# Two attentions of a fused two-block transformer kernel: implied waits dropped, and TensorE's wait for the scaled probabilities moved to the last score matmul

## Chip, cores and metric

One core of one Trainium2 chip. The time is the device time of one launch in microseconds (us), as the median of three runs. The aim of such work is a lower time.

## What is computed

The kernel runs two transformer blocks on a sequence of 1024 tokens of width 1024, all in fp32. Each block holds one attention, and the change touches only these two.

```python
def block_attention(q, k, v):            # first block: 8 query heads, 2 key/value heads of 64
    s = einsum('bqkgd,bskd->bkgqs', qi, k) * scale     # one block of 128 queries, all 1024 keys
    p = softmax(s, axis=-1)
    return einsum('bkgqs,bskd->bqkgd', p, v)
...
def _forgetting_attention(q, k, v, log_f):   # second block: 16 heads of 64, causal
    for blk in range(8):
        q0, q1 = blk * 128, (blk + 1) * 128
        s = einsum('bhqd,bhkd->bhqk', q[:, :, q0:q1], k[:, :, :q1]) * scale
        s = s + fcum[:, :, q0:q1, None] - fcum[:, :, None, :q1]
        s = where(kpos <= qpos, s, -inf)
        outs.append(einsum('bhqk,bhkd->bhqd', softmax(s), v[:, :, :q1]))
```

Around them stand the projections, a token MLP, a gated feed-forward layer with a convolution, and a state space branch.

## The kernel before

Every engine has its own instruction stream, written out by hand in a class of its own, and the streams meet only at semaphores. Each compute engine counts its finished steps up in one semaphore of its own: `pe_done`, `act_done`, `dve_done`, `pool_done`.
Both attentions (A = 1 and A = 2) are one loop over steps s, each of which takes one block of 128 queries of one head, called g. A head has eight blocks. In attention 1 there are 64 blocks of 1024 keys each. In attention 2 there are eight passes (p = 0 to 7) of two heads, so 16 blocks each, with g = 16 p + s, and block qt of a head has (qt + 1) x 128 keys.

One block goes through these steps:

1. `scores` on TensorE (L805, L806): the query tile times the high and the low part of the keys, 512 columns at a time, into one of two PSUM pairs (g % 2). In attention 2 a mask matmul (L810) ends it.
2. `top` on VectorE: the row maximum (L2573; in attention 2 L2568, then L2571 for the sign).
3. `soft` on ScalarE: the exponential with the row sum (L1645), then `soft` on VectorE: the reciprocal of the sum (L2581).
4. `weigh` on GpSimd (POOL, L3451): the probabilities times that reciprocal; its label is `weighed`.
5. `turn` on TensorE (L829): transposes of 128 x 128, at most four to a PSUM bank, so one or two halves. `turn` on ScalarE (L1660, label `phi`) takes a half out as the high part, and then `turn` on VectorE (L2596, label `plo`) as the low part, which frees the bank.
6. `back` on TensorE (L848), for two blocks together: probabilities times values; ScalarE (L1668) and VectorE (L2604) take the result out.

TensorE's order in step s is: `scores` of block s + 2, then, in attention 2, some chunks of a projection matmul as filler (L609 to L611, three matmuls of 512 columns each), then `turn` of block s, then, for every second s, `back` of blocks s - 1 and s - 2. GpSimd has other work in attention 2: it makes the low part of each weight tile (L3374), in its own program order.

Of the kernel before, what the change touches and what calls it, by code (L numbers as in the profile page):

```python
# [545 lines left out]
class TensorEngine(Engine):  # L546
# [243 lines left out]
        self.last_tails()  # L790
        self.mark("stage", "project1")

    def scores(self, A, g, h, qt, q, kh, kl, causal, ready):
        K = self.K
        nk = (qt + 1) * 128 if causal else 1024
        pair = g % 2
        qs = K.wrr(q)[:, qt * 128:(qt + 1) * 128]
        for half in range((nk + 511) // 512):
            c = slice(half * 512, min(nk, half * 512 + 512))
            out = K.ps[pair][:, c]  # L800
            diag = causal and c.stop == nk
            self.bank_free(2 * pair + half)
            for label in ready:
                self.wait_ge(*K.at(*label))
            self.op.matmul(out, qs, K.wrr(kh)[:, c], start=True, stop=False)  # L805
            t = self.op.matmul(out, qs, K.wrr(kl)[:, c], start=False, stop=not diag)  # L806
            if diag:
                self.consts()
                self.wait_ge(*K.at("maskr"))
                t = self.op.matmul(K.ps[pair][:, nk - 128:nk], K.idr[:, :], K.maskr[:, :],  # L810
                                   start=False, stop=True)
        t.then_inc(*self.done("scores", A, g))
        free = (("top", A, g),) if causal else (("top", A, g), ("exp", A, g))
        for half in range((nk + 511) // 512):
            self.emptied[2 * pair + half] = free

    def turn(self, A, g, qt, p, causal):
        K = self.K
        nk = qt + 1 if causal else 8
        par = g % 2 if nk <= 4 else 0  # L820
        self.consts()
        for half in range((nk + 3) // 4):
            bk = (half + par) % 2
            js = range(4 * half, min(nk, 4 * half + 4))
            self.wait_ge(*K.at("weighed", A, g))
            self.bank_free(4 + bk)
            for j in js:
                o = bk * 512 + (j - js[0]) * 128
                t = self.op.transpose(K.ps[2][:, o:o + 128], K.w(p)[:, j * 128:(j + 1) * 128],  # L829
                                      K.c_id)  # L830
            t.then_inc(*self.done("turn", A, g, half))
            self.emptied[4 + bk] = (("phi", A, g, half), ("plo", A, g, half))

    def back(self, A, g, qt, hi, lo, v, causal, ready):

        K = self.K
        nk = qt + 1 if causal else 8
        for gg in (g - 1, g):
            for half in range((((qt if gg == g else qt - 1) + 1 if causal else 8) + 3) // 4):
                self.wait_ge(*K.at("phi", A, gg, half))  # L840
                self.wait_ge(*K.at("plo", A, gg, half))
        for label in ready:
            self.wait_ge(*K.at(*label))
# [10 lines left out]
    def attend1(self):  # L854
        K = self.K

        def sc(s):
            h, qt = s // 8, s % 8
            k = 8 if h < 4 else 10
            self.scores(1, s, h, qt, h, k, k + 1, False, (("stacklo", "q", h // 2), ("stacklo", "q", 4),  # L860
                         ("stackhi2", "q", 4, 1)))

        for s in range(-2, 66):
            if s + 2 < 64:
# [356 lines left out]
    def attend2(self):  # L1221
        K = self.K
# [35 lines left out]
        for p in range(8):  # L1258
# [11 lines left out]
            def sc(s):  # L1270
                h = s // 8
                k = 2 + 2 * h
                self.scores(2, 16 * p + s, 2 * p + h, s % 8, h, k, k + 1, True,
                            (("stacklo", "q2", p, h), ("stacklo", "k", p, h),
                             ("stackhi2", "k", p, h)))

            for s in range(-2, 18):
                if s + 2 < 16:
# [97 lines left out]
class ScalarEngine(Engine):  # L1376
# [251 lines left out]
    def soft(self, A, g, qt, p, causal):  # L1628
# [1 line left out]
        nk = (qt + 1) * 128 if causal else 1024  # L1630
        m, den = (K.st[:, 4 * (g % 16) + j:4 * (g % 16) + j + 1] for j in range(2))
        pw = K.w(p)[:, 0:nk]
        self.wait_ge(*K.at("top", A, g))
        if causal:
            self.wait_ge(*K.at("minus", A, g))
        else:
            self.wait_ge(*K.at("scores", A, g))
            if g >= 4:
                for half in (0, 1):
                    self.wait_ge(*K.at("turn", A, g - 4, half))  # L1640
            else:
                self.wait_ge(*K.at("tok", 2 if g < 2 else 3))
        if g >= 16:
            self.wait_ge(*K.at("weighed", A, g - 16))
        self.op.activation(pw, pw if causal else K.ps[g % 2][:, 0:nk], ACT.Exp, bias=m, scale=1.0,  # L1645
                           accum_out=den).then_inc(*self.done("exp", A, g))

# [638 lines left out]
class VectorEngine(Engine):  # L2286
# [268 lines left out]
    def top(self, A, g, h, qt, p, causal):  # L2555
# [2 lines left out]
        m = K.st[:, 4 * (g % 16):4 * (g % 16) + 1]  # L2558
        ps = K.ps[g % 2][:, 0:nk]
        self.wait_ge(*K.at("scores", A, g))  # L2560
        if g >= 16:
            self.wait_ge(*K.at("exp", A, g - 16))
        if causal:
            pw = K.w(p)[:, 0:nk]
            if g >= 3:
# [9 lines left out]
    def soft(self, A, g):  # L2575
        K = self.K
        den, rd = (K.st[:, 4 * (g % 16) + j:4 * (g % 16) + j + 1] for j in (1, 2))
        self.wait_ge(*K.at("exp", A, g))
        if g >= 16:
            self.wait_ge(*K.at("weighed", A, g - 16))  # L2580
        self.op.reciprocal(rd, den).then_inc(*self.done("rd", A, g))  # L2581

    def turn(self, A, g, qt, parts, causal):
# [4 lines left out]
        for half in range((nk + 3) // 4):  # L2588
# [2 lines left out]
            src = v3(K.ps[2][:, bk * 512:bk * 512 + len(js) * 128])  # L2591
            q = slice((qt % 2) * 128, (qt % 2) * 128 + 128)
            r = slice(js[0], js[-1] + 1)
            self.wait_ge(*K.at("turn", A, g, half))
            self.wait_ge(*K.at("phi", A, g, half))
            self.op.tensor_tensor(lo[:, r, q], src, hif[:, r, q],  # L2596
                                  ALU.subtract).then_inc(*self.done("plo", A, g, half))
# [766 lines left out]
class GpSimd(Engine):  # L3364
# [78 lines left out]
    def weigh(self, A, g, qt, p, causal):  # L3443
# [2 lines left out]
        nk = (qt + 1) * 128 if causal else 1024  # L3446
        rd = K.st[:, 4 * (g % 16) + 2:4 * (g % 16) + 3]
        pw = K.w(p)[:, 0:nk]
        self.wait_ge(*K.at("exp", A, g))
        self.wait_ge(*K.at("rd", A, g))  # L3450
        self.op.tensor_scalar(pw, pw, rd, 0.0, ALU.mult,  # L3451
                              ALU.add).then_inc(*self.done("weighed", A, g))
# [900 lines left out]
```

## Time and profile before

| | |
|---|---|
| median of 3 runs | 2622.48 us (2622.33 to 2622.82) |
| span of the profiled execution | 2619.9 us |
| TensorE busy with matmuls | 97% of the span |
| VectorE, ScalarE, GpSimd busy | 61%, 47%, 43% |
| granted TensorE clock, mean | 0.991 of 2.4 GHz |
| attention 1 | about 255 to 463 us |
| attention 2 | about 1855 to 2341 us |

The span runs from the first to the last instruction of one profiled execution; the 2.6 us between it and the median are the launch around it, and the two are not the same execution.

### The profile page before, as it was taken

What the parts mean: (1) busy time and instruction counts of PE and PEld (TensorE: products, weight loads), DVE (VectorE), ACT (ScalarE), POOL (GpSimd) and SP (SyncE); (2) the same over time, 40 slices, a digit from 0 to 9 for tenths busy, and PEclk for the clock granted to TensorE, in tenths of its full rate; (3) what the DMA queues carried; (4) which work ended last, traced back from release to release, by engine and by line L of the source; (5) the groups of instructions that cost most, each with busy time, mean ns of one, the idle gap of its engine ahead of it and who ended that gap; (6) DMA issues with size and microseconds to landing.
All of it is one profiled execution on the core that took longest, in us unless ns stands there. A gap on an engine that the chain in (4) does not pass through costs nothing.

```text
span 2619.9 us, 33861 instructions
## 1 busy us (share of the span) xinstructions
PE 2539.2 (97%) x12946; PEld 2112.9 (81%) x12946; DVE 1587.0 (61%) x2413; ACT 1233.5 (47%) x1858; POOL 1132.0 (43%) x754
## 2 busy tenths in 40 slices
PE   5999999999999999999999999999999999999998
PEld 3788788777888888878788888888888888888886
DVE  7654889578555566575833366666666666655333
ACT  4343888445444443333533345543656656652132
POOL 0222434437878774444487334233322222235233
PEclk8999999999999999999999999999999999999999
DMA  6134000432222126553233322222111111157342
GB/s 271 65 121 129 1 1 1 142 101 83 94 77 92 73 100 226 192 177 109 107 113 121 121 73 89 81 69 93 57 53 53 49 49 57 60 206 279 146 185 97
DMA packets 84465, 275.89 MB, mean 105 GB/s; under 512 B 9392, under 2 KB 9520, under 8 KB 84304
## 3 DMA queue, kind: packets, MB, share of 16 engines
q1 hardware_dynamic: 84304, 273.71, 29.8%
q8 instruction: 104, 1.70, 0.3%
q14 instruction: 57, 0.47, 0.1%
HBM read 219.54 MB, written 54.13 MB: 104 GB/s over the span
## 4 chain that ended last, share of the span: by engine, by line
PE 81%; DVE 10%; ACT 5%; issue 2%; POOL 1%; DMA 0%; DVEq 0%; SPq 0%; ACTq 0%; POOLq 0%
PE ps L609 12%; PE ps L611 11%; PE ps L610 11%; PE ps L977 7%; PE ps L978 7%; PE ps L979 7%; PE ps L848 5%; PE ps L829 4%; PE ps L1034 3%; PE ps L1036 3%; PE ps L1035 3%; DVE wf L3047 2%; PE ps L805 2%; PE ps L806 2%; DVE st L2573 1%
## 5 line engine op out<-in xcount | busy, mean ns | idle before, releaser
L3374 POOL TENSOR_TENSOR hl<-raw,hl 128x1024 fp32r<-128x1024 f32 x161 | 403.6, 2509 | 929.9 <-ACT hl L1393 929.9
L609 PE MATMUL ps<-ht,hl 128*128 128x512 f32 x1552 | 633.7, 408 | 10.5 <-DVE ht L2444 5.4
L611 PE MATMUL ps<-ht,hl 128*128 128x512 f32 x1552 | 608.4, 392 | 0.0
L610 PE MATMUL ps<-ht,hl 128*128 128x512 f32 x1552 | 608.2, 392 | 0.0
L609 PEld LDWEIGHTS ps<-ht,hl 128*128 128x128 f32 x1552 | 293.6, 189 | 71.3 <-issue 6.2
L611 PEld LDWEIGHTS ps<-ht,hl 128*128 128x128 f32 x1552 | 293.0, 189 | 63.7
L610 PEld LDWEIGHTS ps<-ht,hl 128*128 128x128 f32 x1552 | 294.0, 189 | 54.2 <-issue 1.7
L3451 POOL TENSOR_SCALAR wf<-wf,st 128x1024 f32<-128x1024 f32 (+2 forms) x192 | 167.9, 874 | 343.1 <-DVE st L2581 287.4
L1393 ACT ACTIVATE hl<-raw 128x1024 fp32r<-128x1024 f32 x163 | 171.4, 1053 | 182.2 <-PE ps L1036 66.5
L2384 DVE TENSOR_TENSOR ps<-ps,wf 128x512 f32<-128x512 f32 x116 | 80.8, 697 | 152.1 <-PE ps L979 151.9
L829 PEld LDWEIGHTS ps<-cst,wf 128*128 128x128 f32 x1088 | 126.6, 141 | 56.2 <-issue 34.4
L829 PE MATMUL ps<-cst,wf 128*128 128x128 f32 x1088 | 157.5, 276 | 13.0 <-DVE ht L2596 12.7
L977 PE MATMUL ps<-wr,hl 128*128 128x512 f32 x384 | 149.7, 390 | 2.0 <-POOL hl L3502 1.4
L2596 DVE TENSOR_TENSOR wr<-ps,wr 128x512 fp32r<-128x512 f32 (+1 forms) x192 | 101.2, 555 | 79.9 <-ACT wr L1660 65.5
L979 PE MATMUL ps<-wr,hl 128*128 128x512 f32 x384 | 149.4, 389 | 0.0
L978 PE MATMUL ps<-wr,hl 128*128 128x512 f32 x384 | 149.4, 389 | 0.0
L1460 ACT ACTIVATE hl<-wf 128x512 fp32r<-128x512 f32 x97 | 60.5, 632 | 178.6 <-PE ps L979 132.3
L1034 PE MATMUL ps<-wr,hl 128*128 128x512 f32 x352 | 137.5, 391 | 3.3 <-POOL hl L3374 1.9
L2859 DVE TENSOR_TENSOR wr<-wf,wr 128x512 fp32r<-128x512 f32 x44 | 95.4, 2178 | 70.7 <-ACT wr L1855 70.6
L1036 PE MATMUL ps<-wr,hl 128*128 128x512 f32 x352 | 137.0, 389 | 0.0
L1035 PE MATMUL ps<-wr,hl 128*128 128x512 f32 x352 | 137.0, 389 | 0.0
L3502 POOL TENSOR_TENSOR hl<-wf,hl 128x512 fp32r<-128x512 f32 x97 | 128.6, 1347 | 14.4 <-ACT hl L1460 14.4
(287 smaller groups left out, 5298.5 us busy)
## 6 DMA issues: line engine op xcount, KB each, us to landing
raw<-in_wst SPq DMA_DIRECT2D x243, 512.0 KB, 4.0
wf<-scratch_rows SPq DMA_DIRECT2D x32, 512.0 KB, 5.0
scratch_g<-wf SPq DMA_DIRECT2D x22, 512.0 KB, 2.6
wf<-scratch_g SPq DMA_DIRECT2D x44, 256.0 KB, 4.4
wf<-in_xT SPq DMA_DIRECT2D x16, 512.0 KB, 8.0
htf<-in_wst SPq DMA_DIRECT2D x16, 512.0 KB, 15.4
scratch_ys<-wr SPq DMA_DIRECT2D x16, 512.0 KB, 4.8
ht<-scratch_ys SPq DMA_DIRECT2D x32, 256.0 KB, 6.0
```

Source lines behind the costliest of these rows:

```text
L609: self.op.matmul(out, wh, xh[:, c], start=(j == 0), stop=False)
L610: self.op.matmul(out, wh, xl[:, c], start=False, stop=False)
L611: t = self.op.matmul(out, wl, xh[:, c], start=False, stop=(j == kt - 1))
L829: t = self.op.transpose(K.ps[2][:, o:o + 128], K.w(p)[:, j * 128:(j + 1) * 128], K.c_id)
L977: self.op.matmul(K.bank(bk), wh[:, c], xh, start=(j == 0), stop=False)
L978: self.op.matmul(K.bank(bk), wh[:, c], xl, start=False, stop=False)
L979: t = self.op.matmul(K.bank(bk), wl[:, c], xh, start=False, stop=(j == 3))
L1034: self.op.matmul(K.bank(n), wh, hi, start=(f == 0), stop=False)
L1035: self.op.matmul(K.bank(n), wh, lo, start=False, stop=False)
L1036: t = self.op.matmul(K.bank(n), wl, hi, start=False, stop=(f == NFF - 1))
L1393: self.op.activation(K.hl[:, u * 2048:u * 2048 + 1024], K.raw[:, i % 3 * 1024:(i % 3 + 1) * 1024], ACT.Copy).then_inc(*self.done("whi", i))
L3374: self.op.tensor_tensor(K.hl[:, u * 2048 + 1024:u * 2048 + 2048], K.raw[:, i % 3 * 1024:(i % 3 + 1) * 1024], hi.bitcast(F32), ALU.subtract ...
```

## The change

Waits that another wait of the same instruction implies are dropped on all four compute engines: `plo` implies `phi` and `exp` implies `scores`, for example. One wait is moved: TensorE waited for `weighed` of block s at its first transpose of that block. Now it waits for it in `scores` of block s + 2, ahead of the low-part matmul of the last 512 columns, which stands earlier in TensorE's program. For the last two blocks of the loop (and of each pass in attention 2) no such scores follow, and the wait stays at the transposes. No arithmetic changes, and no instruction that computes changes its place.

```diff
     def scores(self, A, g, h, qt, q, kh, kl, causal, ready, weighed=None):
...
             self.op.matmul(out, qs, K.wrr(kh)[:, c], start=True, stop=False)
+            if c.stop == nk and weighed is not None:
+                self.wait_ge(*K.at("weighed", A, weighed))
             t = self.op.matmul(out, qs, K.wrr(kl)[:, c], start=False, stop=not diag)
...
-        free = (("top", A, g),) if causal else (("top", A, g), ("exp", A, g))
+        free = (("top", A, g),) if causal else (("exp", A, g),)
...  (TensorE, turn)
-            self.emptied[4 + bk] = (("phi", A, g, half), ("plo", A, g, half))
+            self.emptied[4 + bk] = (("plo", A, g, half),)
...  (TensorE, back)
-                self.wait_ge(*K.at("phi", A, gg, half))
                 self.wait_ge(*K.at("plo", A, gg, half))
...  (TensorE, attend1; attend2 likewise with 16 * p + s - 2)
             self.scores(1, s, h, qt, h, k, k + 1, False, (("stacklo", "q", h // 2), ("stacklo", "q", 4),
-                         ("stackhi2", "q", 4, 1)))
+                         ("stackhi2", "q", 4, 1)), s - 2 if s >= 2 else None)
...  (ScalarE, soft)
-        self.wait_ge(*K.at("top", A, g))
         if causal:
             self.wait_ge(*K.at("minus", A, g))
         else:
-            self.wait_ge(*K.at("scores", A, g))
+            self.wait_ge(*K.at("top", A, g))
             if g >= 4:
-                for half in (0, 1):
-                    self.wait_ge(*K.at("turn", A, g - 4, half))
+                self.wait_ge(*K.at("turn", A, g - 4, 1))
...
-        if g >= 16:
-            self.wait_ge(*K.at("weighed", A, g - 16))
...  (VectorE, top)
-        if g >= 16:
-            self.wait_ge(*K.at("exp", A, g - 16))
...  (VectorE, soft)
-        if g >= 16:
-            self.wait_ge(*K.at("weighed", A, g - 16))
...  (VectorE, turn)
-            self.wait_ge(*K.at("turn", A, g, half))
             self.wait_ge(*K.at("phi", A, g, half))
...  (GpSimd, weigh)
-        self.wait_ge(*K.at("exp", A, g))
         self.wait_ge(*K.at("rd", A, g))
```

TensorE in attention 2, step s = 4 of a pass: the end of the scores of block 6, two filler chunks, and the first transposes of block 4. Before:

```order
L805 MATMUL ps<-wr 128x384
L806 MATMUL ps<-wr 128x384
L810 MATMUL ps<-maskr,idr 128x128
L609 MATMUL ps<-ht,hl 128x512
L610 MATMUL ps<-ht,hl 128x512
L611 MATMUL ps<-ht,hl 128x512
L609 MATMUL ps<-ht,hl 128x512
L610 MATMUL ps<-ht,hl 128x512
L611 MATMUL ps<-ht,hl 128x512
L829 MATMUL ps<-cst,wf 128x128 [waits dve_done,act_done,pool_done]
```

And with the change, where L806 has become L808, L810 L812 and L829 L831:

```order
L805 MATMUL ps<-wr 128x384
L808 MATMUL ps<-wr 128x384 [waits pool_done]
L812 MATMUL ps<-maskr,idr 128x128
L609 MATMUL ps<-ht,hl 128x512
L610 MATMUL ps<-ht,hl 128x512
L611 MATMUL ps<-ht,hl 128x512
L609 MATMUL ps<-ht,hl 128x512
L610 MATMUL ps<-ht,hl 128x512
L611 MATMUL ps<-ht,hl 128x512
L831 MATMUL ps<-cst,wf 128x128 [waits dve_done]
```

The wait for GpSimd (`pool_done`) has moved ahead of eight matmuls: the last score matmul, the mask matmul and the two filler chunks. The wait for ScalarE is gone, and the one for VectorE stays.

VectorE in attention 1, a pair of blocks (L2573 row maximum, L2596 low parts, L2581 reciprocal). Before:

```order
L2573 TENSOR_REDUCE st<-ps 128x1 [waits pe_done]
L2596 TENSOR_TENSOR ht<-ps,ht 128x4x128 [waits act_done,pe_done] x2
L2581 RECIPROCAL st<-st 128x1 [waits pool_done,act_done]
L2604 TENSOR_TENSOR htf<-ps,htf 64x256 [waits act_done]
L2573 TENSOR_REDUCE st<-ps 128x1 [waits pe_done]
```

And with the change, where the same lines are L2569, L2589, L2575 and L2597:

```order
L2569 TENSOR_REDUCE st<-ps 128x1 [waits pe_done]
L2589 TENSOR_TENSOR ht<-ps,ht 128x4x128 [waits act_done] x2
L2575 RECIPROCAL st<-st 128x1 [waits act_done]
L2597 TENSOR_TENSOR htf<-ps,htf 64x256 [waits act_done]
L2569 TENSOR_REDUCE st<-ps 128x1 [waits pe_done]
```

Each instruction has one wait left, which it can carry itself.

TensorE in attention 1, the scores of one block and the transposes of another. Before:

```order
L805 MATMUL ps<-wr 128x512 [waits act_done]
L806 MATMUL ps<-wr 128x512
L805 MATMUL ps<-wr 128x512
L806 MATMUL ps<-wr 128x512
L829 MATMUL ps<-cst,wf 128x128 [waits dve_done,act_done,pool_done]
L829 MATMUL ps<-cst,wf 128x128 x3
L829 MATMUL ps<-cst,wf 128x128 [waits dve_done,act_done]
L829 MATMUL ps<-cst,wf 128x128 x3
```

And with the change:

```order
L805 MATMUL ps<-wr 128x512 [waits act_done]
L808 MATMUL ps<-wr 128x512
L805 MATMUL ps<-wr 128x512
L808 MATMUL ps<-wr 128x512 [waits pool_done]
L831 MATMUL ps<-cst,wf 128x128 [waits dve_done]
L831 MATMUL ps<-cst,wf 128x128 x3
L831 MATMUL ps<-cst,wf 128x128 [waits dve_done]
L831 MATMUL ps<-cst,wf 128x128 x3
```

Here the wait for GpSimd moves by one matmul only, since attention 1 has no fillers, and each half of the transposes keeps only the wait for VectorE.

## Rows read from the trace of the kernel before

**Rows 1.** The page's head: the span and the busy time of each engine.

```profile
span 2619.9 us, 33861 instructions
PE 2539.2 (97%) x12946; PEld 2112.9 (81%) x12946; DVE 1587.0 (61%) x2413; ACT 1233.5 (47%) x1858; POOL 1132.0 (43%) x754
```

**Rows 2.** Stretch, its length, busy us (x) of PE, PEld, DVE, ACT, POOL, granted clock.

```profile
255.00:463.00 208.00, 195.21 (x1309) 165.35 (x1308) 177.47 (x287) 170.70 (x299) 83.84 (x69) 0.99 0.03 11
1855.00:2341.00 486.00, 483.66 (x2850) 415.63 (x2849) 313.72 (x820) 299.88 (x619) 148.93 (x152) 1.00 0.19 63
```

**Rows 3.** Waits, attention 1: TensorE's weight loads; total us, times, longest.

```profile
PEld ps L829 <- issue: 28.2, 46, 3.6
```

**Rows 4.** Waits, attention 2: TensorE's weight loads.

```profile
PEld ps L829 <- issue: 6.2, 17, 0.4
```

**Rows 5.** Timeline of attention 1, one pair: start, length, engine, operation.

```profile
367.03 0.42 PEld L829 LDWEIGHTS ps<-cst,wf 128*128 128x128 f32 x4 [0.74 <-issue]
...
369.95 0.19 ACT L1645 ACTIVATION_READ_ACCUMULATOR wf<-ps,st 128x1 f32 x1
370.17 0.16 DVE L2581 RECIPROCAL st<-st 128x1 f32<-128x1 f32 x1
...
371.17 1.23 DVE L2573 TENSOR_REDUCE st<-ps 128x1 f32<-128x1024 f32 x1
371.60 0.60 ACT L1660 ACTIVATE ht<-ps 128x512 fp32r<-128x512 f32 x1 [0.99 <-PE ps L829]
...
372.42 0.69 DVE L2596 TENSOR_TENSOR ht<-ps,ht 128x512 fp32r<-128x512 f32 x1
...
373.23 0.20 PEld L829 LDWEIGHTS ps<-cst,wf 128*128 128x128 f32 x2 [0.74 <-issue]
373.26 0.30 PE L829 MATMUL ps<-cst,wf 128*128 128x128 f32 x1 [0.33 <-DVE ht L2596]
```

**Rows 6.** Timeline of attention 1, a pair further ahead.

```profile
287.75 0.43 DVE L2604 TENSOR_TENSOR htf<-ps,htf 64x256 f32<-64x256 f32 x1 [0.20 <-ACT htf L1668]
288.26 1.23 DVE L2573 TENSOR_REDUCE st<-ps 128x1 f32<-128x1024 f32 x1
289.41 1.28 DVE L2596 TENSOR_TENSOR ht<-ps,ht 128x512 fp32r<-128x512 f32 x2
```

**Rows 7.** Timeline: a weight load that has a single wait, for VectorE.

```profile
1914.59 1.23 DVE L2395 SCALAR_TENSOR_TENSOR wr<-ps,wr 64x1024 fp32r<-64x1024 f32 x1
...
1915.87 0.19 PEld L805 LDWEIGHTS ps<-wr 128*128 128x128 f32 x1 [0.26 <-DVE wr L2395]
```

**Rows 8.** Timeline of attention 2, pass p = 2, step s = 0.

```profile
1979.28 2.39 POOL L3374 TENSOR_TENSOR hl<-raw,hl 128x1024 fp32r<-128x1024 f32 x1 [16.52 <-ACT hl L1393]
...
1981.44 0.34 PE L806 MATMUL ps<-wr 128*128 128x384 f32 x1
...
1981.64 0.38 POOL L3451 TENSOR_SCALAR wf<-wf,st 128x128 f32<-128x128 f32 x1
```

**Rows 9.** The same pass, step s = 4.

```profile
1989.38 2.40 POOL L3374 TENSOR_TENSOR hl<-raw,hl 128x1024 fp32r<-128x1024 f32 x1
...
1991.67 0.34 PE L806 MATMUL ps<-wr 128*128 128x384 f32 x1
...
1991.76 0.81 POOL L3451 TENSOR_SCALAR wf<-wf,st 128x640 f32<-128x640 f32 x1
```

**Rows 10.** The same pass, step s = 6.

```profile
1996.46 1.02 POOL L3451 TENSOR_SCALAR wf<-wf,st 128x896 f32<-128x896 f32 x1 [1.70 <-ACT wf L1668]
...
1997.31 0.27 PE L806 MATMUL ps<-wr 128*128 128x128 f32 x1
```

**Rows 11.** The same pass, step s = 8: low parts, then transposes.

```profile
2002.99 0.59 ACT L1660 ACTIVATE wr<-ps 128x512 fp32r<-128x512 f32 x1
...
2003.68 0.69 DVE L2596 TENSOR_TENSOR wr<-ps,wr 128x512 fp32r<-128x512 f32 x1 [0.79 <-ACT wr L1660]
...
2004.49 0.14 PEld L829 LDWEIGHTS ps<-cst,wf 128*128 128x128 f32 x1 [0.43 <-issue]
```

More of the change, by code:

```diff
@@ L791, in project1, with scores @@
         self.mark("stage", "project1")
-    def scores(self, A, g, h, qt, q, kh, kl, causal, ready):
+    def scores(self, A, g, h, qt, q, kh, kl, causal, ready, weighed=None):
         K = self.K
@@ L1274, in sc @@
                             (("stacklo", "q2", p, h), ("stacklo", "k", p, h),
-                             ("stackhi2", "k", p, h)))
+                             ("stackhi2", "k", p, h)),
+                            16 * p + s - 2 if s >= 2 else None)
             for s in range(-2, 18):
```

## The prediction

> **What bounds the kernel now.** I read the page's head first, then the two attentions as stretches, then who waits for whom inside each, and last the timelines of single steps. TensorE is busy for 97% of the span [rows 1], so a change pays only where TensorE waits or is made to wait. The two attentions differ in that. Attention 1 has 195.2 us of matmuls in 208 us; attention 2 has 483.7 in 486 [rows 2]. So attention 1 has some 13 us to give, and attention 2 almost nothing: whatever TensorE is newly made to wait for there is added to the time.
>
> The waits say where TensorE stands. In attention 1 its weight loads for the transposes (L829) sit idle for 28.2 us in 46 times [rows 3]; the page names no releaser, since each stands behind several waits. In attention 2 the same group is 6.2 us in 17 times [rows 4].
>
> The timeline of a pair of blocks in attention 1 shows the loop. Pairs begin with a weight load of the transposes at 367.03 and at 373.23, so a pair takes 6.20 us, and each time the load came 0.74 us after the end of the one before it [rows 5]. What it waited for is the bank that VectorE frees, as the row of its matmul at 373.26 says: L2596 begins at 372.42, takes 0.69 us, ends at 373.11, and the load follows at 373.23. Before it stands the maximum, 371.17 to 372.40. So the loop is: transposes, `back` and scores on TensorE, maximum and low parts on VectorE, transposes again. The scaling on GpSimd, which the moved wait is about, is not in this loop.
>
> **The change part by part, attention 1.** (a) VectorE's low part loses a wait. Now: the maximum ends at 372.40, ScalarE's high part at 371.60 + 0.60 = 372.20, and yet L2596 starts at 372.42, 0.22 us after what it waits for. An instruction with one wait starts much sooner: ScalarE's sum ends at 370.14 and the reciprocal starts at 370.17, 0.03 us later [rows 5]. Further ahead in the same loop L2596 starts at 289.41, 0.08 us before the maximum ends (288.26 + 1.23 = 289.49) [rows 6]; that is the floor when no wait delays it. With one wait the bounds are 372.20 + 0.03 = 372.23 and 372.40 - 0.08 = 372.32, so it starts at 372.32, 0.10 us earlier. By the starts of the transposes 13 pairs take 6.19 or 6.20 us like this one, and 12 take 6.07 or 6.08 with L2596 at its floor already. So 13 x 0.10 = 1.3 us.
>
> The row is this: the wait that VectorE has ahead of L2596 costs 0.10 us where the engine is otherwise ready. The Trainium skill (VectorE: DVE Perf Modes, The DRAIN you can't avoid) says that semaphores between VectorE's instructions cost nothing extra, and that one should count instructions and not semaphores. By that rule (a) would be 0.
>
> (b) TensorE's transposes lose ScalarE's wait and GpSimd's, and keep VectorE's. Now VectorE's end to the weight load is 373.11 to 373.23, 0.12 us [rows 5]. A load that has only one wait, for VectorE, starts 0.05 us after it: 1914.59 + 1.23 = 1915.82 to 1915.87 [rows 7]. This is on the loop once in a pair, so 0.07 us in each of some 29 pairs, 2.0 us. It could be nothing, if the 0.12 is not due to the extra waits.
>
> (c) The wait for GpSimd moves ahead of one score matmul. In the regular pairs the scaling is ready 0.6 to 1.4 us before that point; in three irregular ones it is 0.1 to 0.3 us late, and there TensorE waits at the transposes right behind anyway. 0.
>
> (d) The other dropped waits (VectorE's reciprocal, ScalarE's exponential, GpSimd's scaling) stand where the engine has slack. They cost nothing now and bring nothing; what hides them is TensorE's part of the loop. Attention 1: -3.3 us, between 0 (no waiting instruction costs anything) and -6.
>
> **Attention 2, the moved wait.** Here filler chunks stand between the new place and the old one (two chunks and the mask matmul at s = 4), and they were what hid the scaling. What queues behind the wait is all of TensorE: the last score matmul, mask, fillers, transposes; and for them wait VectorE's maximum and ScalarE. So I compare, block by block, the end of `weigh` of block s with the start of the last L806 of block s + 2. From that end to the new start I take 0.05 us to the weight load [rows 7] and 0.03 us from there to its matmul, as from 373.23 to 373.26 [rows 5].
>
> At s = 0 the scaling ends at 1981.64 + 0.38 = 1982.02, and L806 starts at 1981.44 [rows 8]. New start 1982.10, so TensorE stands 0.66 us. The scaling is late because GpSimd makes a weight tile's low part just before it, 1979.28 to 1981.67. At s = 4 it is the same: L3374 from 1989.38 to 1991.78, the scaling to 1991.76 + 0.81 = 1992.57, L806 at 1991.67 [rows 9], so 0.98 us. The stand at s = 0 does not help the one at s = 4: GpSimd's tile waits for ScalarE's half of it, which stands in ScalarE's order behind work on TensorE's results, so all of it moves along. At s = 6 the scaling ends at 1997.48 and L806 starts at 1997.31 [rows 10], 0.25 us late by the same sum. But TensorE comes there 0.98 us later than before, and that block's scores were done long before s = 4's stand, so I take 0 and keep 0.25 as bound. In all other steps the scaling is at least 0.1 us early, and early it stays, as a later TensorE moves nothing of GpSimd's by more than itself. Seven passes read alike; the eighth (p = 7) waits longer at s = 0 and less at s = 4, and p = 0 longer at s = 0. I count all as this one: 8 x (0.66 + 0.98) = 13.1 us.
>
> **Attention 2, the dropped waits.** At s = 8 the high part ends at 2002.99 + 0.59 = 2003.58, L2596 starts at 2003.68 (0.10 after, where one wait takes 0.03), ends at 2004.37, and the transposes' load follows at 2004.49 (0.12, where one wait takes 0.05) [rows 11]. That gives 0.14 us back, and the transposes at s = 6, which stand behind VectorE in the same way, some 0.06. 8 x 0.20 = 1.6 us. It could be nothing, or at most the whole of TensorE's waits for the transposes there, 6.2 us [rows 4].
>
> **The sum.** -3.3 + 13.1 - 1.6 = +8.2 us on a span of 2619.9 [rows 1]; the median before is 2622.48, 2.6 above it, so 2630.7 us. By the skill's rule for VectorE, with (a) at nothing, it would be 1.3 more, 2632.0.
>
> The granted clock is 1.00 in attention 2 and 0.99 in attention 1 [rows 2], the level of 2.4 GHz, and in attention 1 it stays there with TensorE's loads idle 0.74 us in every pair. I expect no change from stands of 1 us.
>
> **The rivals.** (1) VectorE's saving is nothing, as the skill's rule has it, and TensorE's too: +11 to +13 us, 2633.5 to 2636. For it: the 12 faster pairs have the same waits and no delay at L2596. Against it: 0.22 against 0.03 us in one and the same pair [rows 5].
>
> (2) The stands are mostly given back. TensorE waits 6.2 us for its transposes in attention 2 already [rows 4]; if a later TensorE finds VectorE's and ScalarE's work always done, that falls away: 13.1 - 6.2 - 3.3 = +3.6, 2626.1, no difference. Or attention 1 falls to what VectorE's own instructions add up to in a pair, 2 x 1.23 + 2 x 1.28 + 2 x 0.16 + 0.43 = 5.77 us [rows 5, 6], against 6.14 on average: 29 x 0.37 = 10.7 saved, 13.1 - 1.6 - 10.7 = +0.8, 2623.3. Against both: these waits are behind chains that begin on TensorE, and move with it.
>
> (3) The change is faster. It would be attention 1, at TensorE's transposes: VectorE's instructions overlap by 0.08 us and more, so 5.77 is no floor, and if the loop closed up until TensorE never waited, 28.2 us would be had [rows 3]: 13.1 - 1.6 - 28.2 = -16.7, 2605.8. It turns faster when more than 11.5 of the 28.2 go, over three times what (a) and (b) explain. Part of the 28.2 is the ordinary spacing of weight loads, and the loop holds real work for the rest.
>
> (4) The moved wait never binds, since GpSimd is idle enough. Then only the gains are left, -4.9 us, 2617.6. [Rows 8] and [rows 9] speak against it plainly.
>
> **Chances.** The forecast (+5.3 to +11) 0.66; rival 1 (above) 0.10; rival 2, with forecast sums under 5.3, 0.19; rivals 3 and 4 0.05. 0.2% is 5.2 us, which is about what a measurement of this kernel can tell from no change. Slower by more: 0.66 + 0.10 = 0.76; within: 0.19; faster: 0.05. The range from 2625.0 to 2635.5 leaves out some 0.1 on the low side (full give-back, faster) and under 0.1 above. The likeliest case alone spans 2627.8 to 2633.5.
>
> **What would show it.** Attention 1: pairs of about 6.0 us in place of 6.20 and 6.08, the load 0.05 us behind L2596, and L2596 at its floor everywhere. Attention 2: in each pass a new idle of about 0.65 us before the last score matmul at s = 0 and 0.98 at s = 4, released by GpSimd's scaling, and passes about 1.4 us longer; none at s = 6. The attentions' lengths: 1 shorter by 3, 2 longer by 11 to 12. I am wrong if attention 1 shrinks by 10 or more, if the stands at s = 0 and 4 are short, or if new ones appear in other steps because a late score delays the next scaling, which would make each pass lose 2 us or more.

## The result

The changed kernel takes 2634.19 us (median of 4 runs, 2629.69 to 2637.37) against 2622.40 us for the kernel before (4 runs, 2621.79 to 2622.82). The ratio is 1.0042, with a 95% interval of 1.0028 to 1.0056, so it is slower by more than the 0.2% that was named as the bound.

The head of the page of the changed kernel, and from its chain the row with TensorE's lines (part 4; the share of the span that each line holds):

```profile
span 2627.7 us, 32742 instructions
PE 2540.6 (97%) x12946; PEld 2113.0 (80%) x12946; DVE 1588.0 (60%) x2413; ACT 1229.6 (47%) x1858; POOL 1132.8 (43%) x754
...
PE ps L609 11%; PE ps L611 11%; PE ps L610 11%; PE ps L978 7%; PE ps L979 7%; PE ps L980 7%; PE ps L849 5%; PE ps L831 3%; PE ps L1035 3%; PE ps L1037 3%; PE ps L1036 3%; DVE wf L3040 2%; POOL hl L3367 2%; PE ps L808 2%; DVE st L2569 1%
```

The busy times are those of [rows 1] within 1.5 us, ScalarE's within 4. What is new is a line of GpSimd in the chain with 2%: L3367, the low part of a weight tile, which was L3374 before and not among the lines named; all of GpSimd had 1% of that chain. That is the first hint: the chain of work that ends last now passes through GpSimd.

The same two stretches as [rows 2], in the changed kernel (length, then busy us and count of PE, PEld, DVE, ACT, POOL, then granted clock, DMA share, GB/s):

```profile
255.00:463.00 208.00, 195.74 (x1316) 165.36 (x1314) 180.31 (x294) 171.52 (x305) 84.89 (x70) 0.99 0.05 18
1855.00:2341.00 486.00, 474.79 (x2785) 405.64 (x2783) 306.04 (x797) 290.11 (x601) 146.02 (x148) 1.00 0.17 57
```

Attention 1 packs slightly more matmuls into its stretch (1316 for 1309), but the stretches are fixed in time and attention 1 began 3 us earlier in this execution, so that says little. Attention 2 lost some 9 us of matmuls from its own, at the same granted clock of 1.00, the 2.4 GHz level: TensorE stands where it did not.

Who waits for whom, in attention 2 (us in total, times, longest). It answers to [rows 4]:

```profile
PEld ps L808 <- POOL wf L3443: 16.0, 16, 1.4
PE ps L808 <- POOL wf L3443: 9.9, 15, 1.1
PEld ps L831 <- DVE wr L2589: 2.4, 8, 0.3
```

L808 is the last score matmul, L3443 the scaling. Sixteen waits in eight passes are two in each, at s = 0 and s = 4. Of the 6.2 us that TensorE's loads waited for the transposes, 2.4 are left.

And in attention 1, which answers to [rows 3]:

```profile
PEld ps L831 <- DVE ht L2589: 27.8, 61, 3.6
...
PE ps L831 <- DVE ht L2589: 8.0, 17, 3.1
```

The load of the transposes has a single wait now, so the view can name its releaser, and it is the one that the prediction had inferred: VectorE's low part.

A sharper measure than the median is the length of each attention, from its first score matmul to its last `back` matmul, and the time from one pass or pair of blocks to the next, all read from the starts of the matmuls in the profiled execution of each kernel (us). The pass is the median of the seven steps from one pass to the next; the pairs are the regular ones, odd heads (slower before) and even heads apart:

```
                    attention 1   attention 2   pass    pairs, odd / even heads
before                 211.53        492.40     63.07     6.20 / 6.08
changed                209.07        504.69     64.60     6.13 / 6.01
drops only   (e1)      210.70        490.57     62.83     6.13 / 6.01
move only    (e2)      211.41        506.22     64.73     6.20 / 6.07
drops, move in 1 (e3)  209.58        490.57     62.83     6.13 / 6.01
changed again (e4)     209.16        504.73     64.60     6.13 / 6.01
e3, one quadrant (e5)  208.29        490.56     62.83     6.01 / 6.01
scale first  (e6)      209.65        498.05     63.70     6.13 / 6.01
TensorE's drops (e7)   209.32        492.15     63.03     6.13 / 6.02
others' drops (e8)     212.22        491.09     62.90     6.20 / 6.07
e3, read at 0 (e9)     207.68        490.49     62.83     6.01 / 6.01
not at blocks 0, 4 (e10) 209.66      491.46     62.97     6.13 / 6.01
```

Attention 1 became 2.5 us shorter and attention 2 12.3 us longer, together 9.8.

### The profile page after: what moved, and what is told of

Read it like the earlier page. It is cut to its first block, busy times and chain, and to the rows that moved or that the text cites. A ratio compares the mean times of both kernels' runs of the same rounds, so it can differ in the third digit from the quotient of the medians.

```text
span 2627.7 us, 32742 instructions
## 1 busy us (share of the span) xinstructions
PE 2540.6 (97%) x12946; PEld 2113.0 (80%) x12946; DVE 1588.0 (60%) x2413; ACT 1229.6 (47%) x1858; POOL 1132.8 (43%) x754
## 4 chain that ended last, share of the span: by engine, by line
PE 77%; DVE 10%; ACT 7%; POOL 3%; issue 1%; DVEq 0%; ACTq 0%; POOLq 0%
PE ps L609 11%; PE ps L611 11%; PE ps L610 11%; PE ps L978 7%; PE ps L979 7%; PE ps L980 7%; PE ps L849 5%; PE ps L831 3%; PE ps L1035 3%; PE ps L1037 3%; PE ps L1036 3%; DVE wf L3040 2%; POOL hl L3367 2%; PE ps L808 2%; DVE st L2569 1%
## 5 line engine op out<-in xcount | busy, mean ns | idle before, releaser
L3367 POOL TENSOR_TENSOR hl<-raw,hl 128x1024 fp32r<-128x1024 f32 x161 | 404.5, 2514 | 930.4 <-ACT hl L1395 930.1
L3443 POOL TENSOR_SCALAR wf<-wf,st 128x1024 f32<-128x1024 f32 (+2 forms) x192 | 167.7, 873 | 350.7 <-DVE st L2575 350.7
L831 PEld LDWEIGHTS ps<-cst,wf 128*128 128x128 f32 x1088 | 127.2, 141 | 50.4 <-DVE ht L2589 27.8
L831 PE MATMUL ps<-cst,wf 128*128 128x128 f32 x1088 | 158.1, 277 | 9.6 <-DVE ht L2589 8.0
L2589 DVE TENSOR_TENSOR wr<-ps,wr 128x512 fp32r<-128x512 f32 (+1 forms) x192 | 100.7, 552 | 91.0 <-ACT wr L1658 90.8
L1658 ACT ACTIVATE wr<-ps 128x512 fp32r<-128x512 f32 (+1 forms) x192 | 87.2, 490 | 109.8 <-PE ps L831 109.6
```

The lines of the kernel that those rows point to most:

```text
L3367: self.op.tensor_tensor(K.hl[:, u * 2048 + 1024:u * 2048 + 2048], K.raw[:, i % 3 * 1024:(i % 3 + 1) * 1024], hi.bitcast(F32), ALU.subtract ...
```

## The experiments

Beside the experiments the kernel before has medians of 2622.51, 2622.98 and 2623.39 us over 21, 33 and 19 runs, in all from 2618.42 to 2626.94. Single microseconds between medians are therefore within its spread, and the verdicts on mechanisms rest on passes and pairs. Regular pairs repeat to 0.02 us, and passes to 0.05 behind the first, which is 0.05 to 0.5 us longer.

**e1, the dropped waits without the moved one.** In both callers of `scores`:

```diff
-                         ("stackhi2", "q", 4, 1)), s - 2 if s >= 2 else None)
+                         ("stackhi2", "q", 4, 1)))
...
-                             16 * p + s - 2 if s >= 2 else None)
```

> The implied waits are dropped on all engines, and TensorE's wait for the scaled probabilities stays where it was, at the first transpose. Theory (the moved wait costs 13 us in attention 2, the dropped waits give 4 to 5 back): 2617.5 to 2619.5 us, each pass of attention 2 about 0.2 us shorter than the 63.07 of the kernel before, pairs of attention 1 at 6.00 and 6.13 as in the changed kernel. Rival (the dropped waits bring nothing, the pairs are shorter only because the moved wait changes the order of things on TensorE): 2622.4 us, passes of 63.07, pairs of 6.08 and 6.20.

Measured: 2620.75 us, ratio 0.9993 (0.9984 to 1.0002). The pass is 62.83 us, 0.24 below before, and the pairs are 0.07 shorter. So the drops gain as forecast in attention 2 (0.20 per pass), and in the pairs of attention 1 they gain what TensorE's part was forecast to, and no more. The whole attention 1 is only 0.8 us shorter, since its first two pairs took 1.0 us more than before. The median lies above the 2617.5 to 2619.5 us expected, and its interval does not exclude "no change".

**e2, the moved wait without the drops.** The kernel before with this alone:

```diff
+            if c.stop == nk and weighed is not None:
+                self.wait_ge(*K.at("weighed", A, weighed))
```

> The kernel before with only the one wait moved, in both attentions; no wait dropped. Theory: 13 us slower, 2634 to 2636 us in a profiled execution like the one of before (2622.4 + 13.1), with stands of about 0.65 and 0.95 us of TensorE before the last score matmul at s = 0 and s = 4 of each pass, and the pairs of attention 1 unchanged at 6.08 and 6.20. Rival (the stands come from the two parts together, since the dropped waits let ScalarE and GpSimd take up the weight tile earlier): under 2628 us.

Measured: 2636.22 us, at the upper edge of what was expected, ratio 1.0057 (1.0045 to 1.0070), passes 1.66 longer, pairs as before. The loss belongs to the moved wait alone, and all of it to attention 2.

**e3, the drops with the move in attention 1 only** (the argument taken away in the second attention).

> The whole change, but in attention 2 the wait for the scaled probabilities stays at the first transpose; in attention 1 it is moved. Theory: the moved wait costs nothing in attention 1 (margins of 0.6 to 1.4 us in the regular pairs), so this equals the kernel with the dropped waits alone, 2617.5 to 2619.5 us. Rival (three irregular pairs of attention 1, where the scaling is 0.1 to 0.3 us late, cost time too): 0.5 to 1 us above that kernel.

Measured: 2618.85 us, ratio 0.9986 (0.9977 to 0.9994). Attention 2 is that of e1 to the hundredth. In attention 1 the regular pairs are equal, so the moved wait costs nothing there. The whole attention is 1.1 us shorter than in e1, which sits in its first two pairs (8.63 and 7.1 us in e1, 7.74 and 6.8 here).

**e4, the changed kernel a second time,** as it is, to see whether the stands vary from one execution to another.

> The changed kernel unchanged, for the spread of its times: its four executions lay between 2629.7 and 2637.4 us, while those of the kernel before lay within 1.1 us. Theory A (the spread comes from that launch's conditions and not from the kernel): all within 1 us of each other and near 2630.3, the profiled span plus the sum. Theory B (the stands differ from execution to execution, because what they wait for hangs on when a weight tile lands): spread of several us again, and in a profile of a longer execution the stands are longer.

Measured: 2633.64 us (2631.16 to 2637.44), ratio 1.0045 (1.0032 to 1.0059). Its pass is 64.60 again, so the stands are the same in these two executions. Theory A is wrong: a spread of some 6 us is there, as in the kernel before, which has one of 8 us. Where it comes from is not shown. Both traced executions are among the shortest of their kernel (2629.69 and 2631.18 us, where others took 2637), so whether the stands are longer in a long one stays open. Outside the attentions there is room for it: between the profiled executions the part from attention 1's end to attention 2's start differs by up to 4.0 us (1385.4 to 1389.4), and the first matmul starts at 19.4 to 21.0 us.

**e5, VectorE's addition in `back` kept to partitions 0 to 63.** L2589 in the changed kernel starts late in odd heads alone. What differs in odd heads is that the addition before it (L2597) works on partitions 64 to 127. On e3, after that addition's wait for `outhi`:

```diff
+        if A == 1:
+            a = slice(0, 64)
```

> On top of the change with attention 2's wait left at the transposes. In attention 1 VectorE's addition in back (L2604 before) reads and writes partitions 0 to 63 for every head, not 64 to 127 for the odd ones, so the odd heads' low half is added to the wrong rows: that part of the result is left wrong. Theory Q (L2596 starts 0.03 us after the maximum's end in the odd heads, and not 0.08 before it, because the addition before touched SBUF from partition 64, so the first instruction behind that reads from partition 0 again is held until the one before has finished): all pairs at 6.01, none at 6.13, attention 1 shorter by 13 x 0.12 = 1.6 us. Theory W (the slower pairs come from the waits that are left, or from where in the ring of 16 statistics columns a block stands): pairs of 6.13 stay.

Measured: 2617.08 us, ratio 0.9977 (0.9968 to 0.9986), and the pairs of odd heads fall from 6.13 to 6.01 (a few to 6.06 to 6.10). In all 14 odd-head places L2589 now starts as early as in even heads. So the delay at L2589 is due to the addition's partitions, and not to a wait. Attention 1 is 1.3 us shorter than in e3 (1.6 expected).

**e6, GpSimd scales before it makes the weight tile's low part.** On the changed kernel, in GpSimd's order:

```diff
+                if s + 2 < 16:
+                    self.weigh(2, g + 2, (s + 2) % 8, 9 + (g + 2) % 3, True)
...
-                if s + 2 < 16:
-                    self.weigh(2, g + 2, (s + 2) % 8, 9 + (g + 2) % 3, True)
```

> On top of the whole change GpSimd scales in each step of attention 2 first and makes the weight tile's low part after it; before, the tile came first. Theory (the stands at s = 0 and s = 4 are there because the tile's 2.4 us stand ahead of the scaling): the stand at s = 4 goes (the reciprocal is ready at 1990.68, so the scaling would end at 1991.5, before the matmul at 1991.67), at s = 0 some 0.4 of 0.65 us stay, since the reciprocal comes late there, and some of s = 6's 0.25 us appears; passes of 63.4 to 63.7 against 64.60, 2630.2 - 8 = 2622 to 2625 us. Rival (the stands come from the length of the chain scores, maximum, exponential, reciprocal, scaling alone): passes stay at 64.6.

Measured: 2627.69 us, ratio 1.0021 (1.0012 to 1.0030), which is 3 us above the 2622 to 2625 expected; pass 63.70, the upper edge, and 0.90 below the changed kernel. Its waits in attention 2, and its timeline at the last score matmul of steps 0 and 4 of a pass:

```profile
PEld ps L808 <- POOL wf L3443: 8.6, 15, 1.4
...
PE ps L808 <- POOL wf L3443: 4.6, 8, 1.1
```

```profile
1983.13 2.40 POOL L3367 TENSOR_TENSOR hl<-raw,hl 128x1024 fp32r<-128x1024 f32 x1 [16.74 <-ACT hl L1395]
...
1985.51 0.37 POOL L3443 TENSOR_SCALAR wf<-wf,st 128x128 f32<-128x128 f32 x1
...
1985.93 0.45 PE L808 MATMUL ps<-wr 128*128 128x384 f32 x1 [0.47 <-POOL wf L3443]
```

```profile
1995.36 0.80 POOL L3443 TENSOR_SCALAR wf<-wf,st 128x640 f32<-128x640 f32 x1 [1.44 <-DVE st L2575]
...
1996.12 2.40 POOL L3367 TENSOR_TENSOR hl<-raw,hl 128x1024 fp32r<-128x1024 f32 x1
...
1996.26 0.39 PE L808 MATMUL ps<-wr 128*128 128x384 f32 x1
```

At s = 4 the scaling now runs ahead of the tile, and L808 starts 0.18 us after L805 as it did before. Its weight load still comes 0.17 us late in seven of the eight passes, which are seven of the 15 waits above, and sets the next matmul back by 0.05 us. At s = 0 the tile (1983.13 to 1985.53) is still ahead of it: that tile is issued before the loop over s, which this edit does not touch, so my expectation for that place (0.4 us left) was wrong: L808 starts 0.80 us after L805, as in the changed kernel. By the starts of the matmuls the 0.87 us that a pass still loses to e1 are 0.73 at s = 0 and the rest at s = 4 and 6. So the stand whose cause was moved away is gone: at s = 4 the tile ahead of the scaling is what makes TensorE stand. At s = 0 no run moved the tile away. There the reciprocal is late too; in the changed kernel:

```profile
1979.16 0.16 DVE L2575 RECIPROCAL st<-st 128x1 f32<-128x1 f32 x1 [0.56 <-ACT wf L1643]
```

It is ready at 1979.32, and the scaling starts at 1979.63, so by these rows the tile holds the scaling some 0.3 us at most, about half of that stand of 0.63. The rest is the chain of scores, maximum, exponential and reciprocal itself. At s = 4 the reciprocal is ready 1.1 us before the scaling starts.

**e7 and e8, whose dropped waits bring what.** e7 is the kernel before with TensorE's three edits alone; e8 is e1 with those three undone:

```diff
-        free = (("top", A, g),) if causal else (("top", A, g), ("exp", A, g))
+        free = (("top", A, g),) if causal else (("exp", A, g),)
...
-            self.emptied[4 + bk] = (("phi", A, g, half), ("plo", A, g, half))
+            self.emptied[4 + bk] = (("plo", A, g, half),)
...
-                self.wait_ge(*K.at("phi", A, gg, half))
```

> The kernel before with only TensorE's implied waits dropped. Theory (of the saving in attention 1 all, and of that in attention 2 most, is TensorE's 0.12 against 0.05 us from VectorE's end to its weight load): pairs of 6.13 and 6.01, passes 0.1 to 0.2 us shorter than 63.07. Rival (the saving is VectorE's): pairs of 6.20 and 6.08.

> The kernel before with the implied waits dropped on VectorE, ScalarE and GpSimd, and not on TensorE. Theory: pairs of 6.20 and 6.08 as before, since those engines' extra waits end before the instruction could start anyway; passes 0.05 to 0.1 us shorter than 63.07 (VectorE's 0.10 against 0.03 us at s = 8). Rival (my prediction's step on VectorE, 0.10 us in 13 pairs): pairs of 6.10 in place of 6.20.

Measured: e7 2622.02 us, 0.9994 (0.9985 to 1.0003); e8 2621.31 us, 0.9996 (0.9987 to 1.0005). In attention 1 the 0.07 us per pair are all in e7 and none in e8. In attention 2 it is the other way round: e7 shortens the pass by 0.04 us, e8 by 0.17. I had expected 0.1 to 0.2 from e7 and 0.05 to 0.1 from e8. Both medians are within the spread.

**e9, only the read moved to partition 0.** On e3; ScalarE's half of `back` writes its result for odd heads to partitions 0 to 63 of a free tile, and VectorE's addition reads it there. It still writes to partitions 64 to 127:

```diff
+        to = K.bsb[0:64, 0:256] if A == 1 and h % 2 else out[a, c]
+        self.op.activation(to, K.ps[3][0:64, 0:256],
...
+        hi = K.bsb[0:64, 0:256] if A == 1 and h % 2 else out[a, c]
+        self.op.tensor_tensor(out[a, c], K.ps[3][64:128, 0:256], hi,
```

> On top of the change with attention 2's wait left at the transposes. In attention 1 ScalarE's half of an odd head's result goes to partitions 0 to 63 of a small tile that is free by then, and VectorE's addition takes it from there and writes the sum to partitions 64 to 127: the whole result is computed. Theory Q' (what holds L2596 is that VectorE's last SBUF read began at partition 64; its last write does not matter, since the maximum in between writes from partition 0 anyway): no pairs of 6.13, all at 6.01, attention 1 as long as with the addition at partition 0 throughout (208.3 us), 2616 to 2618 us. Rival (the write to partition 64 is what holds): pairs of 6.13 stay, 2618.9 us.

Measured: 2617.19 us, ratio 0.9975 (0.9965 to 0.9985), all regular pairs 6.01. VectorE's timeline in an odd head of e9 (the addition is L2598 here, `bsb` the free tile):

```profile
368.50 0.43 DVE L2598 TENSOR_TENSOR htf<-ps,bsb 64x256 f32<-64x256 f32 x1
369.01 1.23 DVE L2569 TENSOR_REDUCE st<-ps 128x1 f32<-128x1024 f32 x1
370.15 0.68 DVE L2589 TENSOR_TENSOR ht<-ps,ht 128x512 fp32r<-128x512 f32 x1
```

L2589 starts 0.09 us before the maximum ends (369.01 + 1.23 = 370.24). In the changed kernel, below, it starts 0.02 us after that end. Both hold in all 14 odd-head places of attention 1. VectorE's write is where it was, and what moved is its read (with it ScalarE's write, to the free tile): the read decides, not the write. Attention 1 is 1.9 us shorter than in e3. e9 beats both kernels of this study's question: 0.25% below the kernel before.

**e10, the moved wait for all blocks but 0 and 4 of each head.** In the second attention of the changed kernel:

```diff
-                            16 * p + s - 2 if s >= 2 else None)
+                            16 * p + s - 2 if s >= 2 and s not in (2, 6) else None)
```

> The whole change, but for blocks 0 and 4 of each pass of attention 2 the wait for the scaled probabilities stays at the transposes; the other twelve of fourteen are moved. Theory (the cost is in these two blocks alone, with up to 0.25 us at block 6 where the stand before it is gone): passes of 62.85 to 63.1, against 62.83 with no wait moved and 64.60 with all. Rival (a moved wait costs something at every block, by the wait on the weight load itself): passes of 63.5 or more.

Measured: 2621.84 us, ratio 0.9989 (0.9980 to 0.9998), pass 62.97, and no wait of L808 for GpSimd is left in its list, which leaves out idle times under 0.15 us. Two of fourteen moved waits make 1.63 of the 1.77 us per pass that the move costs on top of the drops; the other twelve cost 0.14. By the starts of the matmuls all of that is at s = 6: the last score matmul starts 0.20 us after the one before it instead of 0.14, and the next 0.17 after that instead of 0.11, in seven of eight passes. The prediction had kept 0.25 us there as a bound and taken 0, since the stand at s = 4 covers it; in the changed kernel both spacings are as before.

## Why the prediction was right, and where it was off

**The sum.** Forecast +8.2 us, made of -3.3 in attention 1 and +11.5 in attention 2. The profiled executions show -2.5 and +12.3, +9.8 together. In attention 2 that is +14.1 for the moved wait (changed against e1), where the sum had 13.1, and -1.8 for the drops, where it had 1.6. The medians differ by 11.8. The span grew by 7.8 us only, since in that one execution attention 1 began 3.1 us earlier than in the one before, the last part was 0.8 longer and the middle 0.3. These parts the change does not touch, and they differ by as much between other executions, so I count the 2 us between 9.8 and 11.8 as spread; no run shows where they lie.

**The moved wait in attention 2: right, but for 0.10 us behind each stand.** The places [rows 8] and [rows 9] speak of, in the changed kernel:

```profile
1979.26 0.33 PE L805 MATMUL ps<-wr 128*128 128x384 f32 x1
1980.06 0.45 PE L808 MATMUL ps<-wr 128*128 128x384 f32 x1 [0.47 <-POOL wf L3443]
1980.34 0.22 PE L812 MATMUL ps<-maskr,idr 128*128 128x128 f32 x1
```

```profile
1990.23 0.34 PE L805 MATMUL ps<-wr 128*128 128x384 f32 x1
1991.34 0.44 PE L808 MATMUL ps<-wr 128*128 128x384 f32 x1 [0.78 <-POOL wf L3443]
1991.62 0.22 PE L812 MATMUL ps<-maskr,idr 128*128 128x128 f32 x1
```

and GpSimd ahead of the second:

```profile
1988.11 2.40 POOL L3367 TENSOR_TENSOR hl<-raw,hl 128x1024 fp32r<-128x1024 f32 x1
1990.49 0.80 POOL L3443 TENSOR_SCALAR wf<-wf,st 128x640 f32<-128x640 f32 x1
```

From L805 to L808 it was 0.17 us in both places before. Now it is 0.80 and 1.11, so 0.63 and 0.94 where the forecast had 0.66 and 0.98. At s = 4 the scaling ends at 1991.29 and the matmul starts 0.05 us later, not 0.08. What the sum lacked is the matmul behind: L812 follows 0.28 us after L808, where 0.18 was the spacing before. A matmul whose weights come only when its wait ends pushes its successor by 0.10 us more; it does so at all 16 stands, 1.6 us. The stands themselves are 12.5 us in all, with the one at s = 0 longer in passes 0 and 7 and the one at s = 4 shorter in pass 7, as the prediction had said. With it a pass should lose 0.63 + 0.94 + 0.20 = 1.77 us, and that is the difference between 64.60 and 62.83. That the stand at s = 0 does not shorten the one at s = 4 held, and so did the 0 at s = 6, where TensorE's score matmuls follow without a gap. The reason that the prediction gave for the stand at s = 0, the tile just ahead, covers about half of it (rows under e6). Rival 4, the wait that never binds, falls with these rows.

**The dropped waits in attention 2: right in size, not in whose they are.** Forecast 0.20 us per pass, measured 0.24. I worked it out at s = 8 from both engines. Now ScalarE's end to VectorE's start is 0.04 us by the rounded rows (2002.61 + 0.59 = 2003.20 to 2003.24), where I took 0.03. VectorE's end to TensorE's load is 0.05 us (2003.24 + 0.69 = 2003.93 to 2003.98), as forecast:

```profile
2002.61 0.59 ACT L1658 ACTIVATE wr<-ps 128x512 fp32r<-128x512 f32 x1
...
2003.24 0.69 DVE L2589 TENSOR_TENSOR wr<-ps,wr 128x512 fp32r<-128x512 f32 x1 [0.72 <-ACT wr L1658]
```

```profile
2003.98 0.14 PEld L831 LDWEIGHTS ps<-cst,wf 128*128 128x128 f32 x1 [0.31 <-DVE wr L2589]
```

But e7 and e8 put 0.04 of it on TensorE's drops and 0.17 on the other engines'. By the starts of the matmuls e8 is 0.10 us or a little more ahead of before at the transposes of s = 6 and another 0.07 at those of s = 8. The 0.07 is VectorE's step of the forecast: wherever VectorE stood idle for ScalarE in attention 2, its low part starts 0.10 us behind ScalarE's end before and in e7, and 0.03 us in e1, e8 and the changed kernel. The forecast's 0.06 at s = 6 was taken for TensorE's and is the other engines'; which of their waits it is stays open. Of the 6.2 us of waits in [rows 4], 2.4 remain. Rival 2 took that as given back; it was not, since the pass lost the full price of the stands.

**(b), TensorE's load in attention 1: right in size, but read at the wrong load.** The forecast took the load of the first half of the transposes, 0.12 us behind VectorE's low part. In the changed kernel that load's idle fell from 0.74 to 0.68 us, and it comes 0.06 us behind (367.86 + 0.69 = 368.55 to 368.61):

```profile
366.09 0.43 DVE L2597 TENSOR_TENSOR htf<-ps,htf 64x256 f32<-64x256 f32 x1 [0.25 <-ACT htf L1666]
366.61 1.23 DVE L2569 TENSOR_REDUCE st<-ps 128x1 f32<-128x1024 f32 x1
367.86 0.69 DVE L2589 TENSOR_TENSOR ht<-ps,ht 128x512 fp32r<-128x512 f32 x1
```

```profile
368.61 0.14 PEld L831 LDWEIGHTS ps<-cst,wf 128*128 128x128 f32 x1 [0.68 <-DVE ht L2589]
```

But that is not what shortens the pair. In e1 and e7 this first load keeps the wait for GpSimd beside the one for VectorE, still comes 0.12 us behind with an idle of 0.74, and the pairs are the same 0.07 us shorter. What all three kernels share is the load of the second half, which lost its wait for ScalarE. Here are the two low parts as one row (x2) and the second half's four loads (x4), first in the kernel before, then in e7, with the first half's loads between them, then in the changed kernel. The first of these rows names ScalarE as releaser, but VectorE's end is the last one ahead of the load:

```profile
372.42 1.29 DVE L2596 TENSOR_TENSOR ht<-ps,ht 128x512 fp32r<-128x512 f32 x2
373.83 0.42 PEld L829 LDWEIGHTS ps<-cst,wf 128*128 128x128 f32 x4 [0.18 <-ACT wf L1645]
```

```profile
370.52 1.29 DVE L2595 TENSOR_TENSOR ht<-ps,ht 128x512 fp32r<-128x512 f32 x2
371.32 0.31 PEld L829 LDWEIGHTS ps<-cst,wf 128*128 128x128 f32 x3 [0.74 <-issue]
371.86 0.42 PEld L829 LDWEIGHTS ps<-cst,wf 128*128 128x128 f32 x4
```

```profile
367.86 1.29 DVE L2589 TENSOR_TENSOR ht<-ps,ht 128x512 fp32r<-128x512 f32 x2
369.20 0.42 PEld L831 LDWEIGHTS ps<-cst,wf 128*128 128x128 f32 x4 [0.17 <-DVE ht L2589]
```

Behind the end of the second low part the load comes after 0.12 us before (373.71 to 373.83) and after 0.05 in the other two (371.81 to 371.86, 369.15 to 369.20), and from the start of the low parts to it 1.41 us have become 1.34. It is so in every pair of these traces where the load waited. The size came out because both loads have the same step, 0.12 to 0.05; for the first half's load it pays nothing, and the wait for GpSimd dropped there is worth nothing. Nearly all regular pairs are 0.07 us shorter (two stay at 6.19), and the pairs behind the first two give 1.7 us together, where the forecast had 2.0.

**(a), VectorE's low part in attention 1: wrong, 0 where I had 1.3 us.** The step that failed is "With one wait the bounds are 372.20 + 0.03 = 372.23 and 372.40 - 0.08 = 372.32". In the rows above, L2589 has its wait dropped and still starts 0.02 us after the maximum's end (366.61 + 1.23 = 367.84), just where it started before. In an even head it starts ahead of that end (372.74 + 1.22 = 373.96):

```profile
372.74 1.22 DVE L2569 TENSOR_REDUCE st<-ps 128x1 f32<-128x1024 f32 x1
373.88 0.68 DVE L2589 TENSOR_TENSOR ht<-ps,ht 128x512 fp32r<-128x512 f32 x1
```

L2589 starts behind the maximum's end in all 14 places of odd heads where a maximum stands in front, before and after alike, and in no even head. I read one delay as the price of a wait because the two fell together in time. The prediction had the counter-evidence in its own text: the 12 faster pairs have the same waits and no delay. They are the even heads. e5 and e9 show the cause: in odd heads the addition, VectorE's last reader of SBUF, read from partition 64, and L2589 reads SBUF from partition 0. It is then held until the instruction in front of it has finished. The maximum between them reads PSUM alone and does not change this. The Trainium skill states such a rule (VectorE: DVE Perf Modes, Two Vector instructions with no wait between them): an instruction is held when an input starts in another group of 32 partitions than the last read of the same memory did. By it e9 has to end the delay, and it does, 6.13 to 6.01 us. The Trainium skill's rule on semaphores that the prediction weighed (VectorE: DVE Perf Modes, The DRAIN you can't avoid) gave 0 for (a), and was the better forecast there. It does not carry over to a wait that comes last: at s = 8 of attention 2 VectorE started 0.10 us after ScalarE's end with two waits and starts 0.03 us after it with one.

Rival 1 gave 2633.5 to 2636, and the median lies in it, but not by its mechanism: VectorE's saving in attention 1 was nothing, as it said, but TensorE's was there, and what brought the total up to it is the 0.10 us behind each stand (1.6 us) and 2 us that I count as spread between executions.

**(c), (d): right** in the regular pairs. e3 against e1 shows nothing for the move, e8 nothing for the others' drops (an irregular pair and the attention's end are 0.08 us shorter in e8 each). Attention 1 as a whole gained 0.7 us beyond the other pairs' 1.7, all in its first two pairs. These take 7.74 and 7.0 us before, 8.3 and 5.8 in the changed kernel, and 8.6 and 7.1 in e1 and e8. What sets them stays open; no experiment here was aimed at it. Rival 3 would have needed 11.5 us or more from attention 1, and is gone with the pairs at 6.0.

## What to carry to other kernels

A wait may be moved ahead only as far as its releaser is early at every single step: list, step by step, the releaser's end against the new place, and expect the loss at the few steps where that engine has a long instruction just ahead, or where the chain behind it is itself only just in time. Dropping an implied wait pays a few hundredths of a microsecond each time its instruction is the one that the bounding loop waits for, and here paid nothing elsewhere, not even at the load just before that one. Before a delay is charged to a wait, look for the same instruction with the same wait and no delay, and ask what else differs.

## What the runs showed of the hardware

VectorE held the low part until the maximum in front had finished when it read SBUF from partition 0 after a read of SBUF from partition 64: it starts 0.02 us after the maximum's end, and 0.09 us before it when both reads start at partition 0. This is 0.12 us for each regular pair of an odd head; a free tile for one half of the reads removes it, and attention 1 is 1.9 us shorter for it (e9 against e3). An addition that only writes to partition 64 has no such price here.

A TensorE matmul that waited itself, with its weight load, cost the stand and 0.10 us more at the next matmul (0.28 us between them for 0.18, at all 16 stands). Where only its load was late, by 0.17 us, the next matmul came 0.05 us late (e6, s = 4). A load of the transposes released by its only wait starts 0.05 to 0.06 us after the releaser's end, and one with a further wait ahead of it 0.12 us after. VectorE's low part at s = 8 starts 0.03 us after ScalarE's end with one wait and 0.10 us with two.
